# Activations' high part stored at a pitch of 260 fp32 instead of 256 for each contraction tile

## The chip, the cores and the metric

The kernel runs on one core of one Trainium2 chip. The metric is device microseconds for one execution of the whole program.

## The reference

The input x has 256 rows (tokens) of 2048 fp32 values. Two blocks follow each other:

```
# first block
h = x
h = h + gla_mixer(rmsnorm(h, gla_norm), gla_w_in, ..., gla_w_out)
h = h + relu(rmsnorm(h, mlp_norm) @ mlp_w_up)**2 @ mlp_w_down    # 2048 -> 8192 -> 2048
h = rmsnorm(h, final_norm)
# second block
proj = rmsnorm(h, norm_gain_2) @ w_in_2                          # 2048 -> 6144
y = concat(stick_breaking_attention(q, k, v) * silu(g_sb), rg_lru(conv(x_lru)) * silu(g_lru))
out = h + y @ w_out_2
```

Nearly all of the arithmetic is multiplication of a 256-row activation by a weight matrix: gla_w_in (2048 x 6160), gla_w_out (2048 x 2048), mlp_w_up and mlp_w_down (2048 x 8192 and 8192 x 2048), w_in_2 (2048 x 6144) and w_out_2 (2048 x 2048).

## The kernel before

Weights stream through the core in panels of 512 output columns and 2048 contraction rows; there are 64 panels in a fixed order written out as the string KINDS, one letter for each. A panel is 8 chunks, a chunk is CK = 2 contraction tiles of 128 rows: one DMA of 512 KB brings it into one of four slots of raw (SyncE's queue), ScalarE copies it rounded into w_hi (line 706, type fp32r), and VectorE puts the rest, raw minus w_hi, into w_lo (line 1003).

The activations are kept turned, with the contraction along the partitions: KT = 16 contraction tiles of S = 256 tokens. There are two sets, each with a high and a low part: xa_hi and xa_lo feed the panels of the kinds k, q, v, r, u, x, K, Q, V, g and l (40 of 64), xb_hi and xb_lo feed o, d, D and f (24 of 64). TensorE turns 128x128 blocks into PSUM (tp, line 447), ScalarE writes the high part (xa_hi at line 717, xb_hi at lines 713 and 850) and VectorE the low part (lines 1015 and 1010).

The function multiply does one chunk: for each of 2 contraction tiles and each of 2 token tiles, three matmuls into the same accumulator of 512 columns, with 128 tokens of the activation as the stationary operand and 512 columns of the weight as the moving one:

```
pe.matmul(o, xh[:, kt, xs], w_hi[:, n % RING, k, :], start=kt == 0, stop=False)
pe.matmul(o, xh[:, kt, xs], w_lo[:, n % RING, k, :], start=False, stop=False)
last = pe.matmul(o, xl[:, kt, xs], w_hi[:, n % RING, k, :], start=False, stop=kt == KT - 1)
```

These are lines 418, 419 and 420; the first chunk of all has a function of its own (multiply_first, line 435). A chunk has 12 matmuls, a panel 96, the kernel 64 x 96 = 6144 of them; 40 x 32 = 1280 of each of the three lines' kind use the set xa. The function gate_low (line 482) uses xa_hi and xa_lo the other way round, as a moving operand of 256 columns, 16 times each.

Smaller work is put between chunks by hand (after on TensorE, before on the other engines): turning, the scores and the recurrence of the mixers, their norms. Buffers are allocated one behind the other in a partition: raw, w_hi, w_lo, xa_hi, xa_lo, xb_hi, xb_lo, h, stage, and then the small ones. From the program's own allocation raw begins at byte 16,512, w_hi at 32,896, xa_hi at 65,664, xa_lo at 82,048, ident_r at 156,800, below at 157,312 and rows at 158,944. An area named arena (also for gate_w at 221,120 and sp_hi at 226,240 and sp_lo at 222,144) has a fixed place at byte 163,776, behind all of them; the last small buffer ends at 163,392. Inside arena, lru_x has rows at a pitch of 259 fp32 and conv begins 36,912 bytes in.

Of the kernel before, what the change touches and what calls it, by code (L numbers as in the profile page):

```python
# [5 lines left out]
F32R = mybir.dt.float32r  # L6
# [4 lines left out]
P = 128  # L11
D = 2048
S = 256
TT = S // P
KT = D // P
N = 512
CK = 2
CH = KT // CK
RING = 4
EPS = 1e-6  # L20
CHUNK = 64
GH = 4
# [58 lines left out]
def gated_block_kernel(nc, x, gla_norm, gla_w_in, gla_w_gate_up, gla_b_gate, gla_o_norm, gla_w_out,  # L81
# [4 lines left out]
    with ctx:  # L86
        def sb(name, shape, dt=F32):
            return ctx.enter_context(nc.sbuf_tensor(name, shape, dt))

        def sem(name):  # L90
            return ctx.enter_context(nc.semaphore(name))


        raw = sb("raw", [P, RING, CK, N])
        w_hi = sb("w_hi", [P, RING, CK, N], F32R)
        w_lo = sb("w_lo", [P, RING, CK, N], F32R)
        xa_hi = sb("xa_hi", [P, KT, S], F32R)
        xa_lo = sb("xa_lo", [P, KT, S], F32R)
        xb_hi = sb("xb_hi", [P, KT, S], F32R)
        xb_lo = sb("xb_lo", [P, KT, S], F32R)  # L100
# [87 lines left out]

        raw_in = [sem(f"raw_in{i}") for i in range(RING)]
        hi_ready, lo_ready = sem("hi_ready"), sem("lo_ready")  # L190
# [67 lines left out]
        def _(sp):  # L258
            def load(c, n0, it, per, src):

                n = n0 + c
                if it is None:
                    if n >= RING:
                        sp.wait_ge(lo_ready, n - RING + 1)
                elif n >= RING:
# [724 lines left out]
        def _(dve):  # L990
# [41 lines left out]
            def mean(i, src, width):  # L1032

                dve.tensor_scalar(ms[:, i, 0:ST_WIDTH[i]], src, 1.0 / width, EPS, ALU.mult, ALU.add)\  # L1034
                    .then_inc(ms_ready, 1)
# [400 lines left out]
```

## Time and profile before

| | |
|---|---|
| Time, median of 2 runs | 1516.7 us (1515.21 and 1518.2) |
| Profiled execution, span from the first to the last instruction | 1514.3 us |
| Mean granted TensorE clock | 1.000 of full |
| TensorE matmul busy | 1497.6 us, 99% of the span |
| Weight load busy | 1237.1 us, 82% |
| VectorE busy | 843.5 us, 56% |
| ScalarE busy | 711.9 us, 47% |
| DMA | 277.03 MB, mean 183 GB/s |

The profile gives the profiled execution's span, 1514.3 us; its own device time isn't told apart from the two runs. Their median lies 2.4 us above the span. Busy time of matmuls is added up from ends that are modelled, and matmuls overlap, so the distance between their starts says more than the length of one. Idle time of VectorE and ScalarE costs nothing while TensorE goes on.

### The profile page before, as it was taken

The numbers are of one execution on the slowest core, as the hardware profiler recorded it, in microseconds if no ns is written. First come the engines' busy times: TensorE is split into PE (matmuls) and PEld (weight loads), VectorE is DVE, ScalarE is ACT, GpSimd is POOL, SyncE is SP. The second block draws the span as 40 slices with busy tenths as digits, with TensorE's granted clock in tenths as the row PEclk, the third lists the DMA queues.
The fourth block names the chain that finished last, engine by engine and source line by source line (L and its number), as shares of the span: only waits on it lengthen the run. The fifth ranks groups of instructions, "written<-read, shape, count | busy, mean of one in ns | idle before, by whom it ended". The sixth has DMA issues, their size and how long they took to land. (4 is left out here: it accounts for less than half of the span.)

```text
span 1514.3 us, 19184 instructions
## 1 busy us (share of the span) xinstructions
PE 1497.6 (99%) x6826; PEld 1237.1 (82%) x6826; DVE 843.5 (56%) x872; ACT 711.9 (47%) x856; POOL 30.8 (2%) x54
## 2 busy tenths in 40 slices
PE   7999999999999999999999999999999999999998
PEld 6788888888888888888888888888888888888886
DVE  5555545555555545555555554555566776565653
ACT  5544544445444433443344433444654664565532
POOL 3000000000000000000000000000000011000000
PEclk9999999999999999999999999999999999999999
DMA  8455565657666666666666666666556566545564
GB/s 267 137 167 154 145 202 176 187 176 240 192 183 182 192 192 194 185 182 188 194 189 184 189 190 191 189 190 185 182 180 181 154 194 191 166 144 167 181 193 140
DMA packets 144721, 277.03 MB, mean 183 GB/s; under 512 B 10800, under 2 KB 10912, under 8 KB 144512
## 3 DMA queue, kind: packets, MB, share of 16 engines
q1 hardware_dynamic: 143056, 271.75, 59.3%
q0 software_dynamic: 1040, 3.07, 0.6%
q8 instruction: 60, 0.98, 0.3%
q10 hardware_dynamic: 544, 1.05, 0.2%
q14 instruction: 21, 0.17, 0.0%
HBM read 273.74 MB, written 2.10 MB: 182 GB/s over the span
## 5 line engine op out<-in xcount | busy, mean ns | idle before, releaser
L1003 DVE TENSOR_TENSOR w_lo<-raw,w_hi 128x1024 fp32r<-128x1024 f32 x508 | 620.2, 1225 | 610.7 <-ACT w_hi L706 609.3
L706 ACT ACTIVATE w_hi<-raw 128x1024 fp32r<-128x1024 f32 x508 | 537.0, 1059 | 731.7 <-PE acc L420 710.5
L418 PE MATMUL acc<-w_hi,xa_hi 128*128 128x512 f32 x1276 | 506.3, 397 | 1.6 <-issue 1.4
L420 PE MATMUL acc<-w_hi,xa_lo 128*128 128x512 f32 x1276 | 497.3, 390 | 0.0
L419 PE MATMUL acc<-w_lo,xa_hi 128*128 128x512 f32 x1276 | 496.7, 389 | 0.0
L418 PE MATMUL acc<-w_hi,xb_hi 128*128 128x512 f32 x768 | 300.1, 391 | 1.5 <-DVE w_lo L1003 1.5
L420 PE MATMUL acc<-w_hi,xb_lo 128*128 128x512 f32 x768 | 299.0, 389 | 0.0
L419 PE MATMUL acc<-w_lo,xb_hi 128*128 128x512 f32 x768 | 298.8, 389 | 0.0
L418 PEld LDWEIGHTS acc<-w_hi,xa_hi 128*128 128x128 f32 x1276 | 239.7, 188 | 52.0 <-issue 3.2
L420 PEld LDWEIGHTS acc<-w_hi,xa_lo 128*128 128x128 f32 x1276 | 239.5, 188 | 50.7
L419 PEld LDWEIGHTS acc<-w_lo,xa_hi 128*128 128x128 f32 x1276 | 239.9, 188 | 49.4 <-issue 1.9
L418 PEld LDWEIGHTS acc<-w_hi,xb_hi 128*128 128x128 f32 x768 | 144.2, 188 | 31.3 <-DVE w_lo L1003 1.9
L420 PEld LDWEIGHTS acc<-w_hi,xb_lo 128*128 128x128 f32 x768 | 144.2, 188 | 30.2
L419 PEld LDWEIGHTS acc<-w_lo,xb_hi 128*128 128x128 f32 x768 | 144.2, 188 | 29.6
L372 POOL TENSOR_TENSOR rs<-ms,neg_half 128x2 f32<-128x2 f32 (+1 forms) x12 | 14.0, 1163 | 1215.8 <-DVE ms L1034 1215.8
L447 PEld LDWEIGHTS tp<-ident,stage 128*128 128x128 f32 x256 | 29.8, 140 | 4.2
L447 PE MATMUL tp<-ident,stage 128*128 128x128 f32 x256 | 33.1, 272 | 0.0
L1010 DVE TENSOR_TENSOR xb_lo<-tp,xb_hi 128x512 fp32r<-128x512 f32 x40 | 25.6, 681 | 0.0
L1106 DVE TENSOR_TENSOR h<-h,acc 128x1024 f32<-128x1024 f32 x20 | 24.3, 1214 | 0.0
L738 ACT ACTIVATE arena<-h 128x512 f32<-128x512 f32 (+1 forms) x26 | 18.9, 726 | 10.1 <-DVE h L1106 9.7
L1015 DVE SCALAR_TENSOR_TENSOR xa_lo<-tp,par,xa_hi 128x256 fp32r<-128x256 f32 x48 | 20.1, 476 | 3.5 <-ACT xa_hi L717 3.5
L713 ACT ACTIVATE xb_hi<-tp 128x512 fp32r<-128x512 f32 x40 | 21.4, 586 | 0.0
(198 smaller groups left out, 513.1 us busy)
## 6 DMA issues: line engine op xcount, KB each, us to landing
raw<-in_mlp_w_up SPq DMA_DIRECT2D x128, 512.0 KB, 3.7
raw<-in_mlp_w_down SPq DMA_DIRECT2D x128, 512.0 KB, 4.4
raw<-in_gla_w_in SPq DMA_DIRECT2D x96, 512.0 KB, 3.8
raw<-in_w_in SPq DMA_DIRECT2D x96, 512.0 KB, 3.7
raw<-in_gla_w_out SPq DMA_DIRECT2D x32, 512.0 KB, 4.5
raw<-in_w_out SPq DMA_DIRECT2D x32, 512.0 KB, 4.7
result<-stage SPq DMA_DIRECT2D x8, 256.0 KB, 3.3
h<-in_x ACTq DMA_DIRECT2D x2, 512.0 KB, 6.4
```

The costliest lines, as they stand in the source:

```text
L372: pool.tensor_tensor(rs[:, i, 0:w], ms[:, i, 0:w], neg_half[:, 0:w], ALU.pow)\
L418: pe.matmul(o, xh[:, kt, xs], w_hi[:, n % RING, k, :], start=kt == 0, stop=False)
L419: pe.matmul(o, xh[:, kt, xs], w_lo[:, n % RING, k, :], start=False, stop=False)
L420: last = pe.matmul(o, xl[:, kt, xs], w_hi[:, n % RING, k, :], start=False, stop=kt == KT - 1)
L447: last = pe.transpose(tp[:, g % 2, (2 * k + tt) * P:(2 * k + tt + 1) * P], src(k, tt), ident[:, :])
L706: act.activation(w_hi[:, n % RING, :, :], raw[:, n % RING, :, :], ACT.Copy)\
L713: act.activation(dst[:, k0:k0 + 2, :].rearrange("p a b -> p (a b)"), tp[:, bank, :], ACT.Copy).then_inc(tp_hi, 1)
L738: act.activation(junk_to, src, ACT.Square, accum_out=sums[:, col:col + 1])\
L1003: dve.tensor_tensor(w_lo[:, n % RING, :, :], raw[:, n % RING, :, :], w_hi[:, n % RING, :, :].bitcast(F32), ALU.subtract).then_inc(lo_ready, 1)
L1010: dve.tensor_tensor(lo[:, k0:k0 + 2, :].rearrange("p a b -> p (a b)"), tp[:, bank, :], hi[:, k0:k0 + 2, :].rearrange("p a b -> p (a b)").b ...
L1015: ins = dve.scalar_tensor_tensor(out=lo[:, k0 + k, :], in0=tp[:, bank, k * S:(k + 1) * S], scalar=par[:, gain + k0 + k:gain + k0 + k + 1], ...
L1106: dve.tensor_tensor(h[:, :, j * N:(j + 1) * N], h[:, :, j * N:(j + 1) * N], acc[:, b, :, :], ALU.add).then_inc(h_added, 1)
```

## The change

xa_hi gets rows of 260 fp32 (1040 bytes) instead of 256 (1024 bytes), and the kernel uses the first 256 values of each row, through a slice that is taken once at the allocation. Nothing else in the program differs. xa_hi grows by 16 x 16 = 256 bytes in each partition, and the buffers allocated behind it move up by 256 bytes, up to the last small one; arena stays where it is.

```diff
@@ -17,6 +17,7 @@
 CK = 2
 CH = KT // CK
 RING = 4
+PITCH = S + 4
 EPS = 1e-6
 CHUNK = 64
 GH = 4
@@ -94,7 +95,7 @@
         raw = sb("raw", [P, RING, CK, N])
         w_hi = sb("w_hi", [P, RING, CK, N], F32R)
         w_lo = sb("w_lo", [P, RING, CK, N], F32R)
-        xa_hi = sb("xa_hi", [P, KT, S], F32R)
+        xa_hi = sb("xa_hi", [P, KT, PITCH], F32R)[:, :, 0:S]
         xa_lo = sb("xa_lo", [P, KT, S], F32R)
         xb_hi = sb("xb_hi", [P, KT, S], F32R)
         xb_lo = sb("xb_lo", [P, KT, S], F32R)
```

## Rows read from the trace of the kernel before

**Rows 1.** The page: span, busy time, 40 slices (tenths).

```profile
span 1514.3 us, 19184 instructions
PE 1497.6 (99%) x6826; PEld 1237.1 (82%) x6826; DVE 843.5 (56%) x872; ACT 711.9 (47%) x856; POOL 30.8 (2%) x54
...
PE   7999999999999999999999999999999999999998
...
PEclk9999999999999999999999999999999999999999
```

**Rows 2.** Groups by line: count, busy us, mean ns, then idle before and its releaser.

```profile
L1003 DVE TENSOR_TENSOR w_lo<-raw,w_hi 128x1024 fp32r<-128x1024 f32 x508 | 620.2, 1225 | 610.7 <-ACT w_hi L706 609.3
L706 ACT ACTIVATE w_hi<-raw 128x1024 fp32r<-128x1024 f32 x508 | 537.0, 1059 | 731.7 <-PE acc L420 710.5
L418 PE MATMUL acc<-w_hi,xa_hi 128*128 128x512 f32 x1276 | 506.3, 397 | 1.6 <-issue 1.4
...
L418 PEld LDWEIGHTS acc<-w_hi,xa_hi 128*128 128x128 f32 x1276 | 239.7, 188 | 52.0 <-issue 3.2
L420 PEld LDWEIGHTS acc<-w_hi,xa_lo 128*128 128x128 f32 x1276 | 239.5, 188 | 50.7
...
L713 ACT ACTIVATE xb_hi<-tp 128x512 fp32r<-128x512 f32 x40 | 21.4, 586 | 0.0
...
L569 PE MATMUL aux<-arena 128*128 128x256 f32 x32 | 7.6, 379 | 0.0
```

**Rows 3.** Timeline of PE, steady stretch of the set xb (start, length in us).

```profile
508.18 0.39 PE L419 MATMUL acc<-w_lo,xb_hi 128*128 128x512 f32 x1
...
586.65 0.39 PE L420 MATMUL acc<-w_hi,xb_lo 128*128 128x512 f32 x1
```

**Rows 4.** Timeline of PE and PEld, two steady stretches of the set xa.

```profile
250.03 0.39 PE L420 MATMUL acc<-w_hi,xa_lo 128*128 128x512 f32 x1
250.03 0.19 PEld L418 LDWEIGHTS acc<-w_hi,xa_hi 128*128 128x128 f32 x1
...
944.31 0.39 PE L418 MATMUL acc<-w_hi,xa_hi 128*128 128x512 f32 x1
...
974.00 0.39 PE L420 MATMUL acc<-w_hi,xa_lo 128*128 128x512 f32 x1
```

**Rows 5.** Timeline of PE, gate_low with xa as moving operand.

```profile
36.83 0.28 PE L482 MATMUL aux<-xa_lo,gate_w 128*128 128x256 f32 x1
...
38.48 0.28 PE L482 MATMUL aux<-xa_lo,gate_w 128*128 128x256 f32 x1
```

**Rows 6.** Timeline of PE, fp32r matmuls on sp_hi and sp_lo.

```profile
1354.37 0.34 PE L595 MATMUL aux<-sp_lo,below 128*128 128x384 f32 x1
1354.55 0.22 PE L598 MATMUL aux<-sp_hi,neg_ones 128*128 128x128 f32 x1
```

**Rows 7.** Timeline of PE: blocks turned, then conv as moving operand.

```profile
1215.83 1.03 PE L447 MATMUL tp<-ident,stage 128*128 128x128 f32 x8
...
1222.16 1.89 PE L569 MATMUL aux<-arena 128*128 128x256 f32 x8
```

**Rows 8.** Lines 447 and 629: count, min/median/max ns, first and last start.

```profile
L447 PE MATMUL tp<-ident,stage x256: 270/273/273, 107.2 to 1429.1; 128*128 128x128 f32 x128
L447 PEld LDWEIGHTS tp<-ident,h x96: 138/140/230, 5.5 to 1136.3; 128*128 128x128 f32 x96
...
L629 PEld LDWEIGHTS aux<-ident,rows x1: 141/141/141, 30.1 to 30.1; 128*128 128x128 f32 x1
```

**Rows 9.** Writers and readers of xa_hi, by tile, ns.

```profile
L717 ACT ACTIVATE xa_hi<-tp,par x48: 456/472/493, 9.2 to 1137.9; 128x256 fp32r<-128x256 f32 x48
L1015 DVE SCALAR_TENSOR_TENSOR xa_lo<-tp,par,xa_hi x48: 472/476/485, 10.5 to 1139.3; 128x256 fp32r<-128x256 f32 x48
```

**Rows 10.** Timeline of ACT: a write of lru_x, whose pitch is 259.

```profile
1156.82 0.58 ACT L724 ACTIVATE arena<-tp 128x512 f32<-128x512 f32 x1
```

**Rows 11.** Line 1332, which reads lru_x, ns.

```profile
L1332 DVE SCALAR_TENSOR_TENSOR arena<-arena,par x24: 477/479/487, 1165.8 to 1208.6; 128x256 f32<-128x256 f32 x24
```

**Rows 12.** Waits: engine and line, waited for, us, times, longest.

```profile
PE tp L447 <- DMA h<-in_x: 2.2, 1, 2.2
...
PE acc L418 <- DVE w_lo L1003: 1.6, 2, 1.5
PE acc L418 <- issue: 1.4, 2, 0.9
```

## Prediction

> **What bounds the kernel now.** I read the page first. Matmuls fill 99% of the span and every slice but the first and the last; the granted clock is at the full level, 2.4 GHz, throughout; VectorE and ScalarE are about half busy [rows 1]. Busy time of matmuls alone can mislead, so the groups and the waits come next: ScalarE waits 710.5 us for the last matmul of a chunk to free a slot, and VectorE 609.3 us for ScalarE [rows 2], while TensorE itself waits for w_lo only 1.6 us in all at its commonest line, and 2.2 us once for x [rows 12]. So the weights are ready ahead of TensorE everywhere but at the start, and the kernel is as long as TensorE's instructions one after another.
>
> How long is one of them? The listed 397 ns [rows 2] is a latency that overlaps its neighbours. The timeline gives the step from start to start. In a stretch of the set xb the first and the last start shown lie 586.65 - 508.18 = 78.47 us apart, with 346 steps between them (I counted them in the view): 226.8 ns each [rows 3]. In a stretch of the set xa 131 steps take 974.00 - 944.31 = 29.69 us: 226.6 ns [rows 4]. 6144 such matmuls make 6144 x 0.2268 = 1393 us of the 1514.3 us. The other 121 us are blocks turned (368 records, 256 of them from stage, at a step of about 108 ns: 40 us), the small matmuls of the mixers, the first 16 us and the output's tail.
>
> At 2.4 GHz 512 columns are 213.3 ns, so each matmul has 226.8 - 213.3 = 13.5 ns on top of its columns. This is the only thing in the main stream that a different address could take away, and the question of the case is whether addresses make it.
>
> **The change, part by part.** It removes and adds no instruction, wait or DMA. It moves addresses:
>
> (1) The stationary slices of xa_hi. Contraction tile kt begins at 65,664 + 1040 kt instead of 65,664 + 1024 kt. Every slice used to begin at 0 modulo 64 bytes; now it does for a quarter of the tiles only, and the others begin at 16, 32 or 48 modulo 64. Lines 418 and 419 of the set xa load from it: 2 x 1280 = 2560 loads, of which 15/16 = 2400 have a new place relative to the start of xa_hi and 3/4 = 1920 leave the 64-byte grid.
>
> (2) Everything allocated behind xa_hi, xa_lo, xb_hi and xb_lo among it, moves up by 256 bytes. For all these the place modulo 256 stays, the place modulo 512 changes.
>
> (3) ScalarE's writes to xa_hi (48) and VectorE's reads of it (48).
>
> (4) gate_low's 16 moving reads of xa_hi.
>
> Cost of (1). A load runs beside the matmul ahead of it. It begins in the same hundredth of a microsecond as that matmul [rows 4] and takes 188 ns [rows 2], which leaves 226.8 - 188 = 39 ns until the next step. The real room is larger, because loads of this very length also follow one another faster: in gate_low 14 steps take 38.48 - 36.83 = 1.65 us, 117.9 ns each [rows 5], with a 128-column load to each. So a load can go through at least every 117.9 ns, and one of xa_hi would have to take 226.8 - 117.9 = 108.9 ns more before it set the step. No row of before shows an fp32r load off the 64-byte grid. The nearest is the load of rows, fp32, which begins at byte 158,944, 32 modulo 64: 141 ns, where the same kind of load of h on the grid takes 140 [rows 8]. That is 1 ns. If it weren't hidden, 1 ns x 2400 would be 2.4 us; the reverse, 1 ns less, -2.4 us. I take zero, since the cover is 39 ns at least, and keep both ends for the range.
>
> Does the place of the stationary operand relative to the moving one make the 13.5 ns? If it did, the surcharge would depend on it. In the main stream xa_hi's slices and the weights both begin at 128 modulo 512 bytes. In gate_low the stationary gate_w begins at 448 and the moving xa at 128 modulo 512: 117.9 ns for 256 columns (106.7 ns) is a surcharge of 11.2 ns [rows 5]. In the attention the moving sp_lo lies in arena at 448, against below at 128: 1354.55 - 1354.37 = 180 ns for 384 columns (160 ns), 20 ns on top with 10 ns of rounding at either end [rows 6]. So other phases and other pitches carry about the same surcharge, it doesn't grow with the columns, and it is the same for xa_hi, xa_lo, w_hi and w_lo, for every kt. The step of the set xb, with its own addresses, differs from that of xa by 0.2 ns [rows 3, 4]. Plain fp32 matmuls carry less: eight records of 512 column-passes each in conv last 1.89 us in all; less one latency of 379 ns [rows 2] that is 1.51 us for 7 steps, 216 ns, though the moving conv begins at 48 modulo 64 [rows 7]. Eight turned blocks, less 273 ns, take 7 steps of 108 ns [rows 7, 8], a duration in which a 128-column load goes by as well. A surcharge that goes with the fp32r form, and neither with address nor length, isn't touched by a pitch.
>
> A rule of the Trainium skill stands near this. Row first: 226.8 ns per step at 512 columns [rows 3]. TensorE: Matmul & The Clock Gate, section Back-to-back issue gap, gives N / 2.4 + 2.5 ns for a lone stream, 215.8 ns. Were the pitch what keeps the 2400 loads' matmuls from it, 11.0 x 2400 = 26.4 us would go and the time be 1490.3 us; the rows on other phases speak against it, those on conv show that the figure is reached by fp32. The SBUF page (SBUF — State Buffer, Specifications) has lines of 16 bytes; 1040 is a multiple of 16, so by it a slice touches as many lines as before, and the sum would be zero as well; no row shows a 16-byte line.
>
> Cost of (2). All four big buffers keep their place modulo 256. The phases just compared differ by 320 bytes modulo 512 and the surcharge stays, so I take zero. A bound: the whole difference between xa and xb, whose buffers lie at different places, 0.2 ns [rows 3, 4], x 6144 = 1.2 us either way. The weights' DMAs write to raw, which doesn't move; x, which goes to h once at the start, and the eight transfers of the result from stage are the larger ones on moved buffers, and their ends stay on the same grid of 256 bytes.
>
> Cost of (3). ScalarE writes xa_hi in 472 ns, VectorE reads it in an operation of 476 ns [rows 9]. At a pitch of 259 fp32, never mind 260, ScalarE's write of lru_x, 512 values, takes 0.58 us, against 586 ns for xb_hi at 256; VectorE's reads of lru_x take 479 ns, like the 476 of line 1015 [rows 2, 9 to 11]. So at most 7 ns apiece: 48 x 2 x 7 = 0.7 us if all of it were on the path. Only 8 of the 24 pairs of tiles are (panel 0, where TensorE turns x as it goes); the others hide under panels of 22 us. Zero.
>
> Cost of (4): a moving read that begins off the grid. conv, at 48 modulo 64, shows none. 16 x 13.5 ns = 0.2 us at the worst. Zero.
>
> The sum is 0, against the profiled 1514.3 us and the median of 1516.7 us alike. Bounds: 2.4 + 1.2 + 0.7 + 0.2 = 4.5 us upward, 3.6 us downward.
>
> **The rivals.**
>
> Rival A, faster. The stationary stream and the moving stream get in each other's way because all their rows begin at the same place of a power of two, and the pitch spreads them. All of the 13.5 ns goes for 2400 matmuls: 32.4 us, 1484.3 us, 2.1% faster. For it: there is a surcharge, and fp32 matmuls at mixed addresses don't have it. Against it: gate_low and sp have it at other phases, and every kt and both sets have it alike. Chance 3%, some of it with a part of the gain only, inside 2%.
>
> Rival B, slower. The two streams pass each other undisturbed now, since they begin at the same phase, and an fp32r load that begins off the 64-byte grid takes line slots from the moving stream. Its place is lines 418 and 419 in the 40 panels of the set xa; its price is a second surcharge of the size of the first, 13.5 ns x 2400 = 32.4 us, giving 1549.1 us. It decides as soon as the disturbance reaches the moving side at all; a load that is merely longer decides only from 108.9 ns more (39 ns if the load's listed length can't be overlapped). For it: no fp32r load off the grid exists in the trace. Against: rows' load lengthens by 1 ns, conv as a moving operand by nothing. Chance 4%.
>
> Rival C, the change doesn't do what it says. The slice drops out of the access patterns, or the allocator rounds so that the phases come out as they were. The instruction stream is the same then and the time 1516.7 us. Chance 2%; it can't be told from my forecast by time, only by a load that would differ in nothing.
>
> **How the numbers follow.** My forecast, no effect, has 91%, and rivals C, A and B 2, 3 and 4%. The predicted time is 1516.7 us. A measurement of this kernel can tell about 2% from no change, 30 us. The cases within it are the forecast and C, 93%; A gives 3% for faster by more, B 4% for slower by more. The range needs no reach to A and B, which hold 7% together. It takes the bounds of the sum, +4.5 and -3.6 us, and the runs' own spread of 1.5 us about their median: 1516.7 - 5.1 = 1511.6 and 1516.7 + 6.0 = 1522.7; I take 1511.5 to 1522.
>
> **What would show each step right or wrong.** In the trace of the changed kernel the step of a stretch of xa matmuls should be 226.6 ns as in [rows 4], the stretch of xb 226.8 ns as in [rows 3], the loads of line 418 and 419 188 ns (up to 190 would still fit), and lines 717 and 1015 within 10 ns of 472 and 476 ns. Rival A would show the xa stretch near 213 ns per step on two of three matmuls, or 12 steps in 2.61 us; rival B 12 steps in 2.83 us. TensorE's waits should stay as short as in [rows 12]. The prediction is wrong if the 13.5 ns depends on the low bits, between 16 and 64 bytes, of a stationary fp32r address, the one place in which the trace of before has no variation; then the xa panels change in length and the xb panels don't. If both change, it is the shift by 256 bytes.

## The result: 0.9% slower

| | before | changed |
|---|---|---|
| Time, median of 2 runs | 1516.7 us (1515.21, 1518.2) | 1530.99 us (1530.84, 1531.14) |
| Span of the profiled execution | 1514.3 us | 1528.7 us |

The ratio on record is 1.0091, with a 95% interval of 1.0075 to 1.0108 (the two medians divided give 1.0094). The forecast was no change, 1511.5 to 1522 us; the kernel lies 9 us above that range. Two executions at a far lower granted clock, one of the kernel before at 0.78 of full speed and one of the kernel displaced by 16 bytes at 0.56, count in no ratio.

The page of the changed kernel, against [rows 1]:

```profile
span 1528.7 us, 19184 instructions
PE 1513.0 (99%) x6826; PEld 1238.1 (81%) x6826; DVE 843.5 (55%) x872; ACT 712.0 (47%) x856; POOL 30.9 (2%) x54
```

The instructions are as many as before, VectorE, ScalarE and GpSimd are as busy to 0.1 us, and TensorE takes all of the 14.4 us. The changed file has one line more ahead of these functions, so line 418 is now 419, and so on. The groups by line, against [rows 2]:

```profile
L419 PE MATMUL acc<-w_hi,xa_hi 128*128 128x512 f32 x1276 | 511.4, 401 | 0.3 <-issue 0.3
L421 PE MATMUL acc<-w_hi,xa_lo 128*128 128x512 f32 x1276 | 502.8, 394 | 0.0
...
L419 PE MATMUL acc<-w_hi,xb_hi 128*128 128x512 f32 x768 | 300.1, 391 | 1.5 <-DVE w_lo L1004 1.5
L421 PE MATMUL acc<-w_hi,xb_lo 128*128 128x512 f32 x768 | 299.0, 389 | 0.0
...
L419 PEld LDWEIGHTS acc<-w_hi,xa_hi 128*128 128x128 f32 x1276 | 240.2, 188 | 54.9 <-issue 1.9
```

The matmuls of the set xa grew by 4 ns in the listed mean, those on xa_lo too, though xa_lo kept its pitch. Those of the set xb did not change, and a load of xa_hi is still listed with 188 ns. As before, the distance between starts says it better. The same two stretches as in [rows 3, 4], in the timeline of PE; xb first, xa behind it:

```profile
515.83 0.40 PE L420 MATMUL acc<-w_lo,xb_hi 128*128 128x512 f32 x1
...
594.27 0.39 PE L421 MATMUL acc<-w_hi,xb_lo 128*128 128x512 f32 x1
...
954.04 0.39 PE L419 MATMUL acc<-w_hi,xa_hi 128*128 128x512 f32 x1
...
984.29 0.39 PE L421 MATMUL acc<-w_hi,xa_lo 128*128 128x512 f32 x1
```

xb: 78.44 us for 346 steps, 226.7 ns, as before. xa: 30.25 us for 131 steps, 230.9 ns against 226.6. So 4.3 ns are added to a step of these xa panels and nothing to one of xb. 3840 x 4.3 = 16.5 us is a little more than the 14.3 us measured, since the stretch of before leaves out the longer steps that it, too, has where other matmuls come between (below). Over the whole trace (the starts of neighbouring matmuls of one set, up to 260 ns apart, some 3,670 pairs of xa and 2,277 of xb) the mean step of xa is 227.2 ns before and 231.1 ns after the change, that of xb 226.9 ns in both; 3840 x 3.9 = 15.0 us.

Within a panel it doesn't begin at the first tile. This is the start of a panel (contraction tile 0 first, six matmuls to a tile):

```profile
594.49 0.39 PE L419 MATMUL acc<-w_hi,xa_hi 128*128 128x512 f32 x1
...
596.99 0.40 PE L421 MATMUL acc<-w_hi,xa_lo 128*128 128x512 f32 x1
...
600.46 0.40 PE L421 MATMUL acc<-w_hi,xa_lo 128*128 128x512 f32 x1
```

The first 11 steps, tiles 0 and 1, take 2.50 us, 227 ns each. The next 15, from tile 2 on, take 3.47 us, 231 ns each. A block of tile kt of xa_hi begins 16 kt bytes away from the place, modulo 256, where the weights' blocks begin; I call that its distance, and a block with a distance other than 0 displaced.

### The profile page after: what moved, and what is told of

The parts are those of the page before. It is cut to its first block, busy times and chain, and to the rows that moved or that the text cites. A ratio compares the mean times of both kernels' runs of the same rounds, so it can differ in the third digit from the quotient of the medians.

```text
span 1528.7 us, 19184 instructions
## 1 busy us (share of the span) xinstructions
PE 1513.0 (99%) x6826; PEld 1238.1 (81%) x6826; DVE 843.5 (55%) x872; ACT 712.0 (47%) x856; POOL 30.9 (2%) x54
## 3 DMA queue, kind: packets, MB, share of 16 engines
q0 software_dynamic: 1040, 3.07, 0.6%
## 4 chain that ended last, share of the span: by engine, by line
PE 97%; DMA 1%; DVE 1%; SPq 0%; ACT 0%; issue 0%; DVEq 0%; ACTq 0%
PE acc L419 30%; PE acc L421 30%; PE acc L420 30%; PE tp L448 2%; DMA raw<-in_gla_w_in 1%; PE aux L570 0%; DMA result<-stage 0%; DVE w_lo L1004 0%; SPq L268 0%; PE aux L483 0%; PE aux L494 0%; PE aux L502 0%; PE aux L582 0%; PE aux L610 0%; PE aux L514 0%; PE aux L557 0%
## 5 line engine op out<-in xcount | busy, mean ns | idle before, releaser
L1004 DVE TENSOR_TENSOR w_lo<-raw,w_hi 128x1024 fp32r<-128x1024 f32 x508 | 620.1, 1225 | 625.3 <-ACT w_hi L707 623.8
L421 PE MATMUL acc<-w_hi,xa_lo 128*128 128x512 f32 x1276 | 502.8, 394 | 0.0
```

The costliest lines, as they stand in the source:

```text
L1004: dve.tensor_tensor(w_lo[:, n % RING, :, :], raw[:, n % RING, :, :], w_hi[:, n % RING, :, :].bitcast(F32), ALU.subtract).then_inc(lo_ready, 1)
```

## The experiments

Theory T1: a step is longer when the stationary block and the moving block begin at different places modulo 256 bytes. Rivals: T2, two loads that follow each other begin at different places; T3, the shift by 256 bytes of all that follows; and the pitch by itself. All times stand against the kernel before on the same chip, 1516.7 to 1517.3 us in each batch. A step is taken from the same two stretches, 131 steps of xa and 346 of xb, unless it says otherwise; where such a stretch doesn't stand for its trace, the mean over the whole trace stands beside it.

**The shift alone.** `pad` is allocated and never used.

```diff
         xa_hi = sb("xa_hi", [P, KT, S], F32R)
+        sb("pad", [P, 64])
```

> xa_hi keeps its pitch of 256 fp32; a pad of 256 bytes behind it moves xa_lo and all that follows as the change did. Theory T1 (a stationary block that begins 32 to 240 bytes modulo 256 away from where the moving block begins is slower): no stationary block leaves its place modulo 256, so 1516.7 us and steps of 226.7 ns in both sets. Theory T2 (what counts is that two loads that follow each other begin at different places modulo 256): the same, 1516.7 us. Theory T3 (the shift by 256 bytes makes it, through the distance of xa_lo from xa_hi or from the weights): 1531 us, xa steps of 231 ns.

Measured: 1517.47 us, ratio 1.0002 (0.9993 to 1.0012). T3 falls.

**Both parts at a pitch of 260.**

```diff
-        xa_hi = sb("xa_hi", [P, KT, S], F32R)
-        xa_lo = sb("xa_lo", [P, KT, S], F32R)
+        xa_hi = sb("xa_hi", [P, KT, S + 4], F32R)[:, :, 0:S]
+        xa_lo = sb("xa_lo", [P, KT, S + 4], F32R)[:, :, 0:S]
-        rows = sb("rows", [P, P])
+        rows = room(10752, P)
```

> xa_hi and xa_lo both at a pitch of 260 (rows is laid into arena to make room). T1: all three lines of the 40 xa panels load from displaced blocks for contraction tiles 2 to 15; the step of a displaced stretch was about 232 ns with two loads of three displaced, with three of three it is about 234 to 235, so 3840 x 14/16 x 8 ns = 27 us more than before, about 1543 us. T2: hi and lo of one contraction tile begin at the same place again, steps of 226.7 ns, 1516.7 us. T3: 1516 to 1531 us with no dependence on the contraction tile.

Measured: 1531.80 us, ratio 1.0096 (1.0080 to 1.0113). xa steps, PE's timeline:

```profile
953.02 0.39 PE L418 MATMUL acc<-w_hi,xa_hi 128*128 128x512 f32 x1
...
983.29 0.40 PE L420 MATMUL acc<-w_hi,xa_lo 128*128 128x512 f32 x1
```

231.1 ns. T2 falls: the loads agree with each other and the step is as long as in the changed kernel. T1 had the kind right and the size, 1543 us, wrong: a third displaced load of three adds nothing (1531.8 against 1531.0 us). This trace also shows the distances one by one, as means over the 40 panels: 227.2 ns at 0, 228.6 at 16, 229.5 to 233.5 at 32 to 224, and 227.2 at 240 bytes, which is 16 short of 256.

**All activations 128 bytes away.**

```diff
+        sb("pad", [P, 32])
         xa_hi = sb("xa_hi", [P, KT, S], F32R)
```

> Pitch 256 everywhere, but all four activation buffers (and what follows) begin 128 bytes later, so that every stationary block is 128 bytes modulo 256 away from the weights' blocks and no two stationary blocks differ. T1: all 6144 matmuls get the step of contraction tile 8 of the changed kernel (233.2 ns, against 226.7), 6144 x 6.5 ns = 40 us: about 1557 us, and both sets are slow. T2: 1516.7 us, all steps 226.7 ns. T3: no forecast of its own, near 1516.7 us.

Measured: 1549.50 us, ratio 1.0212 (1.0195 to 1.0229). The set xb, untouched by the change itself, is slow now:

```profile
520.21 0.39 PE L420 MATMUL acc<-w_lo,xb_hi 128*128 128x512 f32 x1
...
600.61 0.39 PE L421 MATMUL acc<-w_hi,xb_lo 128*128 128x512 f32 x1
```

80.40 us for 346 steps, 232.4 ns. 5.6 ns x 6144 = 34 us, of which 32.4 are seen; T1 had said 40 us. Every block here begins on the 64-byte grid.

**Only xa_hi 128 bytes away.**

```diff
+        sb("pad", [P, 32])
         xa_hi = sb("xa_hi", [P, KT, S], F32R)
+        sb("pad2", [P, 32])
```

> Pitch 256 everywhere; xa_hi alone begins 128 bytes later within its room, what follows is moved by 256 bytes as in the change. This is contraction tile 8 of the changed kernel for every tile. T1 and T2 alike: xa steps of 233 ns, 3840 x 6.5 ns = 25 us, about 1542 us, set xb unchanged at 226.8. If instead the pitch (or 16-byte granules) and not the place is the cause: 1516.7 us.

Measured: 1539.11 us, ratio 1.0144 (1.0127 to 1.0161), at a pitch of 256. The xa step is 233.4 ns ((987.38 - 956.80) / 131), that of xb 226.8; T1 had 233 ns and 1542 us. So it isn't the pitch but the place.

**Distance or absolute place?** Everything moved together, by a pad of 128 bytes ahead of raw:

> A pad of 128 bytes ahead of raw moves every buffer but the fixed ones of arena, weights and activations alike; all blocks now begin at 0 modulo 256 instead of 128. If the distance between the stationary and the moving block counts (T1), nothing changes in the main stream: 1517 us, steps of 226.7 ns. If the absolute place of the stationary block counts (it must be 128 modulo 256), both sets become slow as when the activations alone were moved by 128: 1549 us, steps of 232 ns.

Measured: 1518.57 us, ratio 1.0008 (0.9999 to 1.0018), steps of 226.7 and 226.8 ns. Then the weights alone moved:

```diff
+        sb("pad", [P, 32])
         w_hi = sb("w_hi", [P, RING, CK, N], F32R)
         w_lo = sb("w_lo", [P, RING, CK, N], F32R)
+        sb("pad2", [P, 32])
```

> w_hi and w_lo begin 128 bytes later, and the activations behind them 256 bytes later, so the moving blocks are displaced and the stationary ones keep their place modulo 256. Distance (T1): 1549 us, steps of 232 ns in both sets, as when the activations were moved. Absolute place of the stationary block: 1517 us. Place of the weights against raw, which ScalarE and VectorE read, as the cause: not told apart from T1 by the time, but then ScalarE's 1059 ns and VectorE's 1225 ns for a chunk would grow.

Measured: 1548.26 us, ratio 1.0207 (1.0190 to 1.0224). Groups by line:

```profile
L1005 DVE TENSOR_TENSOR w_lo<-raw,w_hi 128x1024 fp32r<-128x1024 f32 x508 | 620.2, 1225 | 640.8 <-ACT w_hi L708 639.2
L708 ACT ACTIVATE w_hi<-raw 128x1024 fp32r<-128x1024 f32 x508 | 537.2, 1059 | 762.9 <-PE acc L422 747.0
```

ScalarE and VectorE, whose operands were displaced as well, keep their 1059 and 1225 ns. Of the three engines only TensorE is slower, and what counts is the distance between its two operands.

**Only w_lo moved.** The first pad stands ahead of w_lo instead of w_hi.

> Only w_lo is displaced, by 128 bytes; w_hi and all activations keep their place modulo 256. One moving block of three is then away from the stationary ones. If each pair of a running matmul and the load beside it pays for itself, one step of three grows from 226.7 to 232 ns: 2048 x 5.3 = 11 us, 1528 us, and the steps that follow the matmul on w_lo are the ones. If one displaced stream sets off all three, as the change did with steps on xa_lo: 6144 x 5.3 = 33 us, 1550 us.

Measured: 1546.29 us, ratio 1.0194 (1.0177 to 1.0211); PE's timeline, xb first, xa behind it:

```profile
516.97 0.40 PE L421 MATMUL acc<-w_lo,xb_hi 128*128 128x512 f32 x1
...
597.71 0.39 PE L422 MATMUL acc<-w_hi,xb_lo 128*128 128x512 f32 x1
...
964.09 0.40 PE L420 MATMUL acc<-w_hi,xa_hi 128*128 128x512 f32 x1
...
994.36 0.39 PE L422 MATMUL acc<-w_hi,xa_lo 128*128 128x512 f32 x1
```

The xb step is 233.4 ns here and the xa step 231.1, at one and the same distance; the mean over the whole trace is 232.2 ns in either set, and in xb 233.2, 231.9 and 231.5 ns behind a matmul of line 420, 421 and 422. One moving block of three in a displaced place is enough to lengthen all three steps. A price per displaced pair was the wrong picture.

**The pitch changed, the places not.**

```diff
-        xa_hi = sb("xa_hi", [P, KT, S], F32R)
-        xa_lo = sb("xa_lo", [P, KT, S], F32R)
+        xa = sb("xa", [P, KT, 2, S], F32R)
+        xa_hi, xa_lo = xa[:, :, 0, :], xa[:, :, 1, :]
```

> xa_hi and xa_lo share one buffer, tile by tile: hi at 2048 kt, lo at 2048 kt + 1024. The pitch of each is 512 fp32 instead of 256, but every block begins at the same place modulo 256 as before. T1: 1517 us and 226.7 ns. If a pitch other than 1024 bytes costs by itself: slower, in the xa panels alone, by up to the 14 us of the change.

Measured: 1517.38 us, ratio 1.0002 (0.9992 to 1.0011). A pitch of 512 fp32 costs nothing measurable.

**How small a distance?** Tile 1 of the changed kernel, 16 bytes away, was not slow, and tile 15 of the kernel with both parts at 260, 16 bytes short, wasn't either; so I took distances below 32 bytes for free. First a pitch of 257 for both parts (each followed by a pad of 192 bytes, rows in arena):

> xa_hi and xa_lo at a pitch of 257 fp32, so that contraction tile kt is 4 kt bytes, 0 to 60, away from the place modulo 256 of the weights; pads bring xb back to its place, and rows lies in arena. With 260 the tiles at 0, +16 and -16 bytes kept 226.7 ns and those at 32 and more did not. If the edge lies at 32 bytes, tiles 0 to 7 keep 226.7 ns and tiles 8 to 15 take 232 ns: 8/16 x 3840 x 5.5 ns = 11 us, 1528 us. If it lies just above 16, tiles 0 to 4 keep it: 15 us, 1532 us. If a block that does not begin on a multiple of 16 bytes is slow by itself (one more line of 16 bytes), only tiles 0 and 4 are clean and the time is 1535 us.

Measured: 1535.34 us, ratio 1.0122 (1.0105 to 1.0139); xa step 232.4 ns ((986.83 - 956.39) / 131). The third expectation had this time, but by luck: none of the three had the pattern, and the tiles are slow from the first distance of 4 bytes on. PE's timeline, from the first matmul of tile 0:

```profile
595.67 0.39 PE L420 MATMUL acc<-w_hi,xa_hi 128*128 128x512 f32 x1
...
597.04 0.39 PE L420 MATMUL acc<-w_hi,xa_hi 128*128 128x512 f32 x1
...
599.59 0.39 PE L422 MATMUL acc<-w_hi,xa_lo 128*128 128x512 f32 x1
```

The first six steps take 1.37 us, 228 ns each; from 597.04 on, in tiles 1 and 2, 11 steps take 2.55 us, 232 ns each. Then a constant 16 bytes for everything behind the weights (`sb("pad", [P, 4])` ahead of xa_hi), as I thought:

> All four activation buffers and what follows begin 16 bytes later, off the grid of 64 bytes in every block. By the rule of distances under 32 bytes: 1517 us, all steps 226.7 ns. If what I named in the prediction, a stationary fp32r block off the 64-byte grid, costs anything: slower, up to the 1549 us of a displacement by 128 bytes.

Measured: 1553.05 us, ratio 1.0236 (1.0219 to 1.0253), the slowest of all. PE's timeline, set xb:

```profile
522.52 0.39 PE L420 MATMUL acc<-w_lo,xb_hi 128*128 128x512 f32 x1
...
603.24 0.40 PE L421 MATMUL acc<-w_hi,xb_lo 128*128 128x512 f32 x1
```

233.3 ns. But the run isn't what its expectation says: the allocator rounds the start of a buffer up to a multiple of 32 bytes, so that xa_hi begins at 65,696 and all four activation buffers lie 32 bytes away. It shows that 32 bytes are too many, and not that 16 are.

So the last three runs make one allocation of all four buffers and skip k = 4, 60 or 1 values of it:

```diff
+        acts = sb("acts", [P, k + 4 * KT * S], F32R)[:, k:].rearrange("p (a k s) -> p a k s", a=4, k=KT)
+        xa_hi, xa_lo, xb_hi, xb_lo = (acts[:, a, :, :] for a in range(4))
```

> The four activation buffers are one allocation of which the first 16 bytes are skipped, so that every stationary block is exactly 16 bytes ahead of equal places. If distances up to 16 bytes keep the streams in step: 1517 us, 226.7 ns in both sets. If only equal places do, and tile 1 of the changed kernel was carried along by the tile before it: 1549 to 1553 us, 232 to 233.5 ns.

> The same with 240 bytes skipped, 16 bytes short of equal places modulo 256. If 16 bytes either way are free: 1517 us. If only equal places are: 1549 to 1553 us. Tile 15 of the kernel with both parts at 260 had 226.7 ns here, coming from a slow tile 14, which speaks for the first.

> The same with 4 bytes skipped, so that blocks no longer begin on a multiple of 16 bytes. With the pitch of 257 all tiles from the first were slow, multiples of 16 among them, so that one can't tell a slow place from a step not found again. If distance up to 16 bytes is free whatever the grid: 1517 us. If a start within a piece of 16 bytes costs by itself: 1549 to 1553 us.

Measured, in this order: ratios of 1.0053 (1.0037 to 1.0069; 1524.16 to 1527.69 us in four runs), 1.0027 (1.0018 to 1.0037; median 1521.07 us) and 1.0196 (1.0179 to 1.0213; median 1547.75 us). With 16 bytes, PE's timeline in a stretch of the MLP (51 steps) and behind two matmuls of the recurrence (33 steps):

```profile
515.78 0.39 PE L416 MATMUL acc<-w_hi,acts 128*128 128x512 f32 x1
...
527.34 0.39 PE L416 MATMUL acc<-w_hi,acts 128*128 128x512 f32 x1
...
1236.05 0.39 PE L416 MATMUL acc<-w_hi,acts 128*128 128x512 f32 x1
...
1243.75 0.40 PE L416 MATMUL acc<-w_hi,acts 128*128 128x512 f32 x1
```

11.56 / 51 = 226.7 ns in the one, 7.70 / 33 = 233.3 ns in the other, in the same execution with the same addresses. Neither expectation allowed for that. With 16 bytes' distance there are two ways of running on, and an interruption (other matmuls between those of the panels) decides which; each lasts until the next one. Every uninterrupted stretch of ten or more steps in this trace has 226.6 to 226.8 ns or 233.1 to 233.6 ns, and nothing between. The same kind of stretch 16 bytes short of equal places (51 steps), then 4 bytes away (39 steps):

```profile
699.71 0.39 PE L416 MATMUL acc<-w_hi,acts 128*128 128x512 f32 x1
...
711.36 0.39 PE L416 MATMUL acc<-w_hi,acts 128*128 128x512 f32 x1
```

```profile
702.87 0.39 PE L416 MATMUL acc<-w_hi,acts 128*128 128x512 f32 x1
...
711.93 0.40 PE L416 MATMUL acc<-w_hi,acts 128*128 128x512 f32 x1
```

228.4 ns and 232.3 ns. At 16 bytes short, too, a step has more than one value: the 346 steps of xb, 509.79 to 588.24 us, take 226.7 ns each, and the mean over the trace is 227.7; with 4 bytes it is 232.4. So 16 bytes either way are in part free, and 4 bytes are as dear as 128: not the smallness of the distance counts, but that it is none, or one piece of 16 bytes. This would also be why tile 1 of the changed kernel was spared, coming from tile 0 in step, and why tile 4 of the kernel at 257, likewise 16 bytes away, was not: it came from tiles at 4 to 12 bytes.

What an interruption does can be read in the kernel before itself. Its timeline behind the matmuls of line 569:

```profile
1224.12 0.39 PE L419 MATMUL acc<-w_lo,xa_hi 128*128 128x512 f32 x1
...
1225.51 0.39 PE L419 MATMUL acc<-w_lo,xa_hi 128*128 128x512 f32 x1
...
1226.41 0.39 PE L420 MATMUL acc<-w_hi,xa_lo 128*128 128x512 f32 x1
```

Six steps take 1.39 us, 232 ns each, the next four 0.90 us, 225 ns (rounding is 2 to 3 ns). At equal places, too, some nine steps behind an interruption are longer: in this trace 819 of them have a mean of 229.6 ns, and the 5,132 behind them 226.7. I picture this as two streams of reads, the load's and the moving operand's, that are out of step and find it again; the traces show the steps and not the reads.

**Does the load's size set the 13.5 ns?** The matmuls on w_lo and on the low part load 64 tokens instead of 128. The low parts' products of the other tokens are left out, and the full matmul comes last of the three (indices shortened to [...]).

```diff
-                        pe.matmul(o, xh[:, kt, xs], w_hi[:, n % RING, k, :], start=kt == 0, stop=False)
-                        pe.matmul(o, xh[:, kt, xs], w_lo[:, n % RING, k, :], start=False, stop=False)
-                        last = pe.matmul(o, xl[:, kt, xs], w_hi[:, n % RING, k, :], start=False,
-                                         stop=kt == KT - 1)
+                        half = slice(tt * P, tt * P + P // 2)
+                        if kt == 0:
+                            pe.matmul(o, xh[:, kt, xs], w_hi[...], start=True, stop=False)
+                        pe.matmul(o[0:P // 2, :], xh[:, kt, half], w_lo[...], start=False, stop=False)
+                        last = pe.matmul(o[0:P // 2, :], xl[:, kt, half], w_hi[...], start=False, stop=False)
+                        if kt:
+                            last = pe.matmul(o, xh[:, kt, xs], w_hi[...], start=False, stop=kt == KT - 1)
```

> Addresses as before the change, but the matmuls on w_lo and on the low part of the activations take only the first 64 of each 128 tokens as stationary operand, which leaves the low parts' products of the other 64 tokens out of the result; the full one comes last but in contraction tile 0. If the 13.5 ns on top of the 512 columns is time that the load takes from the moving stream, in proportion to what it reads, two steps of three shrink by half of it, 6.7 ns, to 220 ns: 4096 x 6.7 = 27 us less, about 1490 us. If it is a fixed cost of each fp32r matmul, all steps stay at 226.7 ns and the time at 1517 us.

Measured: 1531.65 us, ratio 1.0092 (1.0075 to 1.0109), xb step 229.5 ns ((594.97 - 515.58) / 346), though a half load is listed with 135 ns instead of 188. Both expectations fail: a proportional share of the load would have shortened the step, and a fixed cost would have left it at 226.7 ns. It fits that fewer columns loaded at equal places put the streams out of step too, as a displacement does, but the order of the matmuls changed as well, and no run tells the two apart.

**Which reads meet?** In the next four the set xa alone repeats one column, so that its results are those of one token or one weight column; the set xb is the control. First the load, at equal places and 128 bytes away (one of three matmuls shown, indices shortened; the other two are changed alike):

```diff
-                        pe.matmul(o, xh[:, kt, xs], w_hi[:, n % RING, k, :], start=kt == 0, stop=False)
+                        pe.matmul(o, xh[:, kt, tt * P:tt * P + 1].to_broadcast([P, P]), w_hi[...], ...)
```

> Places as before the change. In the panels of the set xa the stationary operand is one column of activations repeated 128 times, so every product of these panels is that of one token in place of its tile's 128; the set xb is as before and serves as control. If the load's reads take time from the moving stream (32 pieces of 16 bytes for 128 columns), the xa step falls from 226.7 towards 213.3 to 216 ns: 3840 x 11 to 13 ns = 42 to 51 us less. If the 13.5 ns is a fixed cost of the fp32r form: 226.7 ns and 1517 us.

> As with the repeated stationary column, but all activations are 128 bytes away from the weights modulo 256. If the extra 5 to 6 ns of a displaced block come from a load that reads along beside the moving stream: xa steps as in the undisplaced run with one column, while the xb panels take 232 ns. If the distance costs whatever the load reads: both about 5 ns above the undisplaced run.

Measured: 1526.34 us (ratio 1.0065, 1.0042 to 1.0088) and 1546.36 us (1.0195, 1.0165 to 1.0224). The first at equal places, PE's timeline, in two panels:

```profile
466.99 0.39 PE L420 MATMUL acc<-w_lo,xa_hi 128*128 128x512 f32 x1
...
488.50 0.39 PE L421 MATMUL acc<-w_hi,xa_lo 128*128 128x512 f32 x1
...
950.32 0.40 PE L419 MATMUL acc<-w_hi,xa_hi 128*128 128x512 f32 x1
...
980.60 0.40 PE L421 MATMUL acc<-w_hi,xa_lo 128*128 128x512 f32 x1
```

In the later panel it is 231.1 ns, and 231.1 ns as well 128 bytes away ((995.21 - 964.93) / 131), with the xb steps at 226.7 and 232.4 ns. But in the earlier one 94 steps take 21.51 us, 228.8 ns each, and over the whole traces the xa step has a mean of 230.0 ns at equal places and 231.5 ns 128 bytes away. The times agree: they differ by 20.0 us, and the displaced set xb accounts for only 2304 x 5.6 = 13 us of it. So a load of one column isn't cheaper, as the expectation had it. At equal places its step is longer than that of a walking load (226.7 ns), when displaced a little shorter (232.4 ns), and the distance still matters by some 1.5 ns of 5.6. Now the moving operand:

```diff
-                        pe.matmul(o, xh[:, kt, xs], w_hi[:, n % RING, k, :], start=kt == 0, stop=False)
+                        pe.matmul(o, xh[:, kt, xs], w_hi[:, n % RING, k, 0:1].to_broadcast([P, N]), ...)
```

> Places as before the change. In the panels of the set xa the moving operand is one weight column repeated 512 times, so all 512 output columns are that one; xb as control. If the two streams' reads meet and the moving one reads anew for each column: 226.7 ns as before. If repeated reads of one place are cheaper, or meet the load less: down to 213 to 216 ns. If they meet it more, since they stay in one place: above 226.7.

> As with the repeated moving column, but all activations 128 bytes away. If the distance acts through two streams that both walk along: xa steps as in the undisplaced run with one moving column, xb panels 232 ns. Otherwise xa about 5 ns above it.

Measured: 1480.63 us (ratio 0.9761, 0.9733 to 0.9790) and 1492.35 us (0.9839, 0.9808 to 0.9869). At equal places (101 steps) and 128 bytes away (131 steps):

```profile
929.79 0.38 PE L419 MATMUL acc<-w_hi,xa_hi 128*128 128x512 f32 x1
...
951.64 0.38 PE L421 MATMUL acc<-w_hi,xa_lo 128*128 128x512 f32 x1
```

```profile
932.26 0.38 PE L420 MATMUL acc<-w_hi,xa_hi 128*128 128x512 f32 x1
...
960.59 0.38 PE L422 MATMUL acc<-w_hi,xa_lo 128*128 128x512 f32 x1
```

216.3 and 216.3 ns. Without a moving operand that walks along, the distance costs nothing, and of the 13.5 ns only 3 remain. Whether the other 10 ns come from the load beside it or from the walking reads alone isn't shown: no run leaves the load out. The second kernel's loss against the first, 12 us, is the displaced set xb: 2304 x 5.6 = 13 us.

## Why the prediction was wrong

**What bounds the kernel** held. TensorE's chain of starts is the kernel: with every activation displaced, for instance, the steps' means over the trace (232.5 and 232.4 against 227.2 and 226.9 ns) give 33 us, and 32.4 were measured. The runs with one moving column fit less well: 3840 x 10.9 = 42 us less by the steps against 36 measured; 2 us of the gap are ten steps of 427 ns at a granted clock of 0.50 of full, from 71 to 75 us, and the rest I haven't traced.

**The step that failed** is in the cost of (1), the paragraph "Does the place of the stationary operand relative to the moving one make the 13.5 ns?". It said that other phases carry about the same surcharge and concluded that it goes with the fp32r form. In its place the runs show that the surcharge depends on the distance: 13.4 ns at equal places modulo 256, 19 to 20 at 4, 32 or 128 bytes, and 3 where the moving operand stays in one column. The change put 13 of 16 tiles of xa_hi at distances of 32 to 224 bytes, and the mean xa step became 3.9 ns longer. The evidence was misread three times. That every tile and both sets had the same step [rows 3, 4] was no variation at all, since all their blocks stood 0 modulo 256 apart. gate_low's blocks stand 64 bytes apart modulo 256, but there is no 256-column matmul at equal places to hold its 11.2 ns against [rows 5]. And the 20 ns of sp_lo [rows 6] was what a displaced block costs, put down to rounding. What could have warned me, steps of 0.23 and 0.24 us in turn behind every interruption at the same addresses, I took for rounding too. The pattern that the prediction named as its own refutation came, xa panels longer and xb panels not, but for another quantity: it is the distance between the two operands, and not the low bits of the stationary address (with all buffers moved by 128 bytes the time was 1518.6 us).

**The load's cover**, 39 to 109 ns, was there and beside the point. The load is still listed with 188 ns and nothing waits for it, yet the step beside it is longer, depending on where the load reads.

**Rival B** had the direction, and in the reads that meet once the phases differ the mechanism that the runs fit best. Its place was wrong: the 64-byte grid has no part in it (the runs with 128 bytes stay on it). Its price was too high: 13.5 ns x 2400 against a measured 3.9 ns x 3840, the latter in all three lines of the xa panels and not in two. That put it at 1549 us, and its 4% was far too little. **Rival A** is ruled out: none of the tested distances is faster than none, and 1517 us stays the best of the complete kernels.

**Rival C** is ruled out by the traces: the xa steps changed. **Costs (2), (3) and (4)** at zero held: the shift alone gives 1.0002, and by tile ScalarE's writes to xa_hi and VectorE's reads of it have a median of 471 and 477 ns against 472 and 476 [rows 9]. That the stretches' 16.5 us are 2 us more than the 14.3 us seen goes back for the most part to the longer steps behind the interruptions, which the kernel before has as well: they are why its mean over the trace is 227.2 ns and not 226.6.

**The forecast of the sum**, 0 with bounds of +4.5 and -3.6 us, thus lacked its one large term. The bound of 2.4 us for (1) came from a load's duration where it should have come from a step's: with 20 against 13.5 ns [rows 6] it would have been 6.5 x 2400 = 16 us.

What stays open: whether and where the two reads meet, since no trace shows a read; why a load of 64 columns lengthens the step; why displaced steps of one distance run at different lengths (231.1 and 233.4 ns with w_lo displaced); and what in an interruption decides between the two ways at 16 bytes. gate_low has such a second value too: its steps take 117.7 ns before, and with xa moved by 128 bytes 113.4 ns in one kernel (activations moved) and 117.8 ns in another (everything moved), though gate_w and xa lie alike in both.

## What to carry to other kernels

Where TensorE runs one fp32r matmul behind another, let the stationary and the moving blocks begin at the same place modulo 256 bytes: a row pitch or a pad that isn't a multiple of 256 bytes cost 0.3 to 2.4% here, where such matmuls fill 92% of the time, and one displaced operand of three was enough. Look at the distance between starts, not at listed durations, and over several stretches or the whole trace: a single stretch misleads where w_lo is displaced or one column is loaded. Treat sameness among rows as evidence only where the suspected quantity differs among them. Check from the program's allocation where each buffer really begins; mine was rounded once, and a run meant for 16 bytes measured 32.

## What the runs showed that I had not expected

- The step of an fp32r matmul of 512 columns at the full clock is 226.7 ns at equal places, up to 233.4 ns at others, and 216.3 ns with a moving operand of one column. The last is close to the 215.8 ns that the Trainium skill, TensorE: Matmul & The Clock Gate, Back-to-back issue gap, gives by its formula for 512 columns. The Trainium skill, SBUF — State Buffer, Who interferes with whom, gives TensorE two independent read ports, one for the moving operand and one for loads. The Trainium skill, TensorE: Matmul & The Clock Gate, What happens when you issue a matmul, says that loading doesn't steal read bandwidth from the running matmul. The runs that move one operand against the other (226.7 to 232.4 ns) don't agree with it for fp32r, and the measurement decides: the step depends on where the load reads.
- Where the places agree, the step comes down to 226.7 ns by itself within about nine matmuls after an interruption; at 16 bytes' distance it stays at whichever of two values the interruption left.
- The changed kernel's profiled execution has a short stretch at the lower of the two clock levels, 3.6 us long, which the one of before doesn't have at this place, behind 32 small matmuls of line 502. By stretches, with PE, PEld, DVE, ACT and POOL busy, granted clock, DMA share and GB/s:

```profile
74.00:78.00 4.00, 4.00 (x12) 2.74 (x11) 1.58 (x2) 1.24 (x3) 0.00 (x0) 0.75 0.39 111
```

  Twelve instructions instead of 16 fit into these 4 us; about 1.7 us of the profiled span, and no part of the cause. In the kernel before ten steps among the first twelve matmuls of the panels, from 10.7 us on, also take 427 ns each, which is 512 columns at 1.2 GHz, though the profile shows the granted clock as full there; so "throughout" in the prediction wasn't quite right, without a consequence for the difference.
